# The router product of a two-layer encoder: router as stationary operand, plain fp32 in place of three split products

## The reference, cut to what matters

```python
y = h * rsqrt(mean(h * h) + 1e-6) * g2        # RMSNorm, 1024 frames
logits = y @ w_router                          # (1024, 1024) @ (1024, 8)
top_val, top_idx = top_k(logits, 2)
gates = softmax(top_val)
# each frame goes through the SwiGLU of its two experts (inner width 3584),
# y_e = (silu(y @ Wg[e]) * (y @ Wu[e])) @ Wd[e], weighted by its gates
```

## Time and profile before

| what | value |
|---|---|
| median of 3 runs | 4281.76 us (4280.26 to 4285.87) |
| span of the profiled execution | 4292.7 us |
| own time of the profiled execution | the page gives its span alone |
| busy: TensorE | 3891.8 us (91%) |
| busy: VectorE, ScalarE | 1811.8 us (42%), 1699.0 us (40%) |
| mean granted TensorE clock | 0.936 |

### The profile page before, as it was taken

How to read it: one execution, slowest core, us unless ns; L and a number is a source line. 1 busy time by engine, 2 the same in 40 slices (tenths; PEclk the granted TensorE clock), 3 DMA queues, 4 the chain that set the end, 5 groups by cost and what they waited for, 6 DMA issues and landing times.

```text
span 4292.7 us, 69381 instructions
## 1 busy us (share of the span) xinstructions
PE 3891.8 (91%) x25092; PEld 3517.8 (82%) x25093; DVE 1811.8 (42%) x2616; ACT 1699.0 (40%) x2513; POOL 91.9 (2%) x118
## 2 busy tenths in 40 slices
PE   7888888999999998996599898998999999998994
PEld 5777776688778866875599898997999999998994
DVE  4443434333243233323244453553444545454444
ACT  3333333333233232213354453543545555464543
POOL 1000000000000000001000000000000000000001
PEclk8889878999999999996799999999999999999997
DMA  4000001133323331112545455554555656565556
GB/s 147 26 26 28 23 20 64 61 96 93 93 73 93 93 108 50 34 64 45 143 156 170 151 182 166 185 195 137 164 175 172 197 192 196 193 196 180 167 166 227
DMA packets 149206, 530.78 MB, mean 124 GB/s; under 512 B 17816, under 2 KB 17856, under 8 KB 148752
## 3 DMA queue, kind: packets, MB, share of 16 engines
q1 hardware_dynamic: 126864, 461.95, 33.8%
q0 software_dynamic: 12864, 49.22, 3.3%
q10 hardware_dynamic: 9280, 17.24, 1.3%
HBM read 501.88 MB, written 30.14 MB: 124 GB/s over the span
## 4 chain that ended last, share of the span: by engine, by line
PE 86%; DVE 5%; issue 4%; ACT 2%; DMA 1%; ACTq 0%; POOL 0%; DVEq 0%; POOLq 0%
PE ps L255 28%; PE ps L257 27%; PE ps L256 27%; PE ps L304 1%; PE ps L395 1%; DMA hrow_d<-rows 1%; DVE rstd L286 1%; DVE tb L295 1%; DVE ptl L452 0%; PE ps L961 0%; DMA y<-yrow_d,slot 0%; DVE xl L503 0%; DVE xl L291 0%; ACT prob L472 0%; DVE prob L424 0%
## 5 line engine op out<-in xcount | busy, mean ns | idle before, releaser
L250 DVE TENSOR_TENSOR wl<-wraw,wh 128x1024 fp32r<-128x1024 f32 x864 | 1057.2, 1224 | 1644.8 <-ACT wh L246 1644.5
L246 ACT ACTIVATE wh<-wraw 128x1024 fp32r<-128x1024 f32 x864 | 909.2, 1057 | 1227.4 <-PE ps L257 1219.2
L255 PE MATMUL ps<-exh,wh 128*128 128x240 f32 (+3 forms) x3584 | 1031.3, 288 | 103.9 <-issue 94.2
L256 PE MATMUL ps<-exl,wh 128*128 128x240 f32 (+3 forms) x3584 | 1029.4, 287 | 0.6 <-issue 0.6
L257 PE MATMUL ps<-exh,wl 128*128 128x240 f32 (+3 forms) x3584 | 1029.3, 287 | 0.0
L255 PEld LDWEIGHTS ps<-exh,wh 128*128 128x128 f32 x3584 | 685.0, 191 | 106.1 <-issue 106.1
L257 PEld LDWEIGHTS ps<-exh,wl 128*128 128x128 f32 x3584 | 684.4, 191 | 0.8 <-issue 0.8
L256 PEld LDWEIGHTS ps<-exl,wh 128*128 128x128 f32 x3584 | 684.9, 191 | 0.0
L255 PE MATMUL ps<-mah,wh 128*128 (+4 forms) x1792 | 511.6, 285 | 0.6
L257 PE MATMUL ps<-mah,wl 128*128 (+4 forms) x1792 | 510.8, 285 | 0.0
L256 PE MATMUL ps<-mal,wh 128*128 (+4 forms) x1792 | 510.8, 285 | 0.0
(11 more groups left out here) (234 smaller groups left out, 4837.7 us busy)
## 6 DMA issues: line engine op xcount, KB each, us to landing
wraw<-in_w_expert SPq DMA_DIRECT2D x676, 512.0 KB, 3.4
wraw<-in_w_main SPq DMA_DIRECT2D x188, 512.0 KB, 3.6
yrow_d<-yst ACTq DMA_DIRECT2D x16, 512.0 KB
yT<-in_xT POOLq DMA_DIRECT2D x4, 1024.0 KB, 10.6
hT<-in_xT POOLq DMA_DIRECT2D x1, 4096.0 KB, 13.8
h_d<-hT POOLq DMA_DIRECT2D x1, 4096.0 KB, 13.2
hT<-h_d POOLq DMA_DIRECT2D x1, 4096.0 KB, 12.5
xrow_d<-rows ACTq DMA_DIRECT2D x16, 256.0 KB
```

The costliest lines, as they stand in the source:

```text
L246: act.activation(wh[:, j], wraw[:, j], ACT.Copy).then_inc(hi_done, 1)
L250: dve.tensor_tensor(wl[:, j], wraw[:, j], wh[:, j].bitcast(F32), ALU.subtract).then_inc(lo_done, 1)
L255: pe.matmul(out, a_hi, b_hi, start=first, stop=False)
L256: pe.matmul(out, a_hi, b_lo, start=False, stop=False)
```

## The change

The router block (128 channels x 8 experts) becomes the stationary operand and 512 normed frames move, in plain fp32, straight from `yT`: 16 instructions, 8 for each half, with the logits as 8 partitions x 512 frames in bank 6 (half 0) and bank 4 (half 1). VectorE copies both to the new tile `lgT`; after batch 1 of the row transposes TensorE turns `lgT` back with 8 transposes into bank 6, where the logits stand as before. The high and low parts of the normed frames and of the router are not made any more; the tiles `rwh`, `rwl` and the semaphores `r_hi`, `r_lo` go. ScalarE takes the root of half 0 before the squares of half 1, and TensorE waits block by block (`n_t`) rather than for the last low part.

```diff
--- before.py
+++ after.py
@@ -149,7 +149,7 @@
         s4 = ExitStack()
         sb("under_norm", [P, 3 * KD * T + 6 * HALF], F32, s4)
         rw = sb("rw", [P, KD * NE], F32, s4)
-        rwh, rwl = (sb(n, [P, KD * NE], F32R, s4) for n in ("rwh", "rwl"))
+        lgT = sb("lgT", [NE, T], F32, s4)
         below = sb("below", [P, P], F32, s4)
         tokid = sb("tokid", [P, NT], U32, s4)
         iota8 = sb("iota8", [P, NT, NE], F32, s4)
@@ -217,7 +217,7 @@
         sc, ttr, ex, es, st2, pn = (sem(n) for n in ("sc", "ttr", "ex", "es", "st2", "pn"))
         tr, pt_hi, pt_lo, pv, y_a, y_d = (sem(n) for n in ("tr", "pt_hi", "pt_lo", "pv", "y_a", "y_d"))
         sp_hi, sp_lo, h_in, op_mm, op_add = (sem(n) for n in ("sp_hi", "sp_lo", "h_in", "op_mm", "op_add"))
-        r_in, r_hi, r_lo, lg_mm, lg_cp, r_own, rk_mm = (sem(n) for n in ("r_in", "r_hi", "r_lo", "lg_mm", "lg_cp", "r_own", "rk_mm"))
+        r_in, lg_mm, lg_cp, r_own, rk_mm = (sem(n) for n in ("r_in", "lg_mm", "lg_cp", "r_own", "rk_mm"))
         g_exp, r_cst, slots_ok, items_ok, tok_z, tok_st = (sem(n) for n in ("g_exp", "r_cst", "slots_ok", "items_ok", "tok_z", "tok_st"))
         tr_mm, row_cp, row_st = sem("tr_mm"), sem("row_cp"), [sem(f"row_st{b}") for b in range(ROWS)]
         list_in, x_got, xt_mm, x_hi, x_lo = (sem(n) for n in ("list_in", "x_got", "xt_mm", "x_hi", "x_lo"))
@@ -799,14 +799,14 @@
         def route_pe(pe):
             norm_pe(pe, 6)
             norm_pe(pe, 7)
-            pe.wait_ge(r_lo, 1)
-            for t in range(NT):
-                pe.wait_ge(n_lo, 56 if t < NT // 2 else 64)
-                c = slice(t * P, t * P + P)
+            pe.wait_ge(r_in, 16)
+            for half in range(2):
+                c = slice(half * HALF, half * HALF + HALF)
                 for k in range(KD):
-                    e = slice(k * NE, k * NE + NE)
-                    mm = product(pe, bank(6, NE, t * NE), xh[:, k, c], xl[:, k, c], rwh[:, e], rwl[:, e], k == 0, k == KD - 1)
-            mm.then_inc(lg_mm, 1)
+                    pe.wait_ge(n_t, 8 * (6 + half) + k + 1)
+                    mm = pe.matmul(bank((6, 4)[half])[0:NE], rw[:, k * NE:k * NE + NE], yT[:, k, c],
+                                   start=k == 0, stop=k == KD - 1)
+                mm.then_inc(lg_mm, 1)
             for b in range(32):
                 if b >= 4:
                     pe.wait_ge(row_cp, b - 3)
@@ -814,6 +814,11 @@
                 for i in range(4):
                     mm = pe.transpose(bank(b % 4, P, P * i), src[:, 4 * (b % 2) + i, b % 16 // 2 * P:b % 16 // 2 * P + P], ident[:])
                 mm.then_inc(tr_mm, 1)
+                if b == 1:
+                    pe.wait_ge(lg_cp, 2)
+                    for t in range(NT):
+                        mm = pe.transpose(bank(6, NE, t * NE), lgT[:, t * P:t * P + P], ident[0:NE, 0:NE])
+                    mm.then_inc(lg_mm, 1)
                 if b == 5:
                     pe.wait_ge(r_own, R_SENT)
                     pe.matmul(bank(5, NT * NE), below[:], sent[:].rearrange("p t e -> p (t e)"), start=True, stop=False)
@@ -822,12 +827,12 @@
 
         def route_act(act):
             act.wait_ge(op_add, 32)
-            squares_act(act, 6, hT, 0)
-            squares_act(act, 7, hT, 1)
-            norm_act(act, 6, 0, xdst(0), yT)
-            norm_act(act, 7, 1, xdst(1), yT)
-            act.wait_ge(r_in, 16)
-            act.activation(rwh[:], rw[:], ACT.Copy).then_inc(r_hi, 1)
+            for half in range(2):
+                n = 6 + half
+                squares_act(act, n, hT, half)
+                act.wait_ge(n_squ, 8 * n + 8)
+                act.wait_ge(n_rstd, n)
+                act.activation(rs[:], sums(n), ACT.Sqrt, bias=epsc[:, 0:1], scale=1.0 / D).then_inc(n_rs, 1)
             for b in range(32):
                 t = b % 16 // 2
                 act.wait_ge(tr_mm, b + 1)
@@ -842,10 +847,19 @@
                               rows[:, b % ROWS]).then_inc(row_st[b % ROWS], 16)
 
         def route_dve(dve):
-            norm_dve(dve, 6, hT, 0, 3, xdst(0), yT)
-            norm_dve(dve, 7, hT, 1, 3, xdst(1), yT)
-            dve.wait_ge(r_hi, 1)
-            dve.tensor_tensor(rwl[:], rw[:], rwh[:].bitcast(F32), ALU.subtract).then_inc(r_lo, 1)
+            for half in range(2):
+                n = 6 + half
+                cols = slice(half * HALF, half * HALF + HALF)
+                dve.wait_ge(n_rs, n + 1)
+                dve.wait_ge(n_t, 8 * n)
+                dve.reciprocal(rstd[:], rs[:]).then_inc(n_rstd, 1)
+                dve.wait_ge(n_rstd, n + 1)
+                for k in range(KD):
+                    dve.scalar_tensor_tensor(yT[:, k, cols], hT[:, k, cols], gains[:, 3, k:k + 1], rstd[:],
+                                             ALU.mult, ALU.mult).then_inc(n_t, 1)
+            for half in range(2):
+                dve.wait_ge(lg_mm, half + 1)
+                dve.tensor_copy(lgT[:, half * HALF:half * HALF + HALF], bank((6, 4)[half])[0:NE]).then_inc(lg_cp, 1)
             n = [0]
 
             def own(ins):
@@ -853,7 +867,7 @@
                 n[0] += 1
                 ins.then_inc(r_own, 1)
                 dve.wait_ge(r_own, n[0])
-            dve.wait_ge(lg_mm, 1)
+            dve.wait_ge(lg_mm, 3)
             dve.wait_ge(r_cst, 5)
             own(dve.tensor_copy(lg[:].rearrange("p t e -> p (t e)"), bank(6, NT * NE)))
             for t in range(NT):
```

## The result

The changed kernel takes 4216.49 us in the median (4213.56 to 4222.31, 4 runs) against 4283.18 for the kernel before, measured again beside it in 4 runs; the ratio is 0.9838, 95% interval 0.9825 to 0.9851: 66.7 us less, where 52.2 were predicted.

The account below looks back on a forecast made before the run. Bound: router stage, 30.1 us of TensorE idle while VectorE makes blocks, then a 41.2 us product at clock 0.50. Norm, product and turning back bring the logits 52.2 us earlier: 4281.8 - 52.2 = 4229.6 us, range 4216 to 4248.

Parts of the forecast that it names:

- The stage: Router stage from the norm's squares to the logits' copy: logits can be copied 52.2 us earlier, at 1959.7 instead of 2011.90.
- Turning back: After the router product: eight transposes of `lgT` on TensorE, bounded by 0.7 and 2.6 us, taken as 1.3.
- faster than summed: Rival, router product: 8-column weight loads and ready blocks remove its gap, ending up to 4.4 us sooner; 4225, 8%.
- The bound for the low clock: Router product at low clock throughout, 30.2 us, ending 1972.3; as a rival 34.3 us saved, 4247.5, 12%.
- The clock: Router product: TensorE comes from the sums without a break and stays at 1.00, 0.93 us an instruction.
- an 8-column side loses the clock: Rival, router product: 8-column stationary side leaves the clock low from about its start; 34.3 us saved, 4247.5, 12%.
- The join: List load, where row stream (about 54 us earlier) meets the tokens' path (52.2): the later one's shift, 52.2, counts.
- The experts: Experts' stretch after the router: expected to stay as long as the 2195.8 us of before.
- a smaller drift of the same kind: Experts' items: pauses at their starts may shift by 10 us in all either way, kept in the range.
- slower than before: Rival, experts' item starts: shorter code moves what follows; all eight pauses at 21.6 cost 78.4 us more, 4308.0; 3%.
- the floor case: Router product ends at VectorE's floor, up to 4.4 us sooner; 4225, 8%; with a drift of 9 the range's bottom.

Follow-up runs that it names:

- product_only: Changed kernel with the norm of before: both roots after both halves' squares, high and low parts still made; 4250.1 us, ratio 0.9916.
- frames_stationary: Changed kernel with the product's sides swapped back, 128 frames stationary and 8 router columns moving, plain fp32, no lgT; 4224.6 us, ratio 0.9860.
- pad_act: Changed kernel with 15 more semaphore increments on ScalarE before its row copies, nobody waiting for them; 4232.1 us, ratio 0.9877.
- before_act113: Kernel before the change with 113 semaphore increments added on ScalarE, while it idles during the router product; 4268.7 us, ratio 0.9963.

## Why the prediction was wrong

**The stage, right.** 52.2 us were summed, 54.4 measured. By steps, from the first square: root of half 0, 8.3 us predicted, 8.3 measured; first blocks at 12.4 and 12.4; last block of half 1 at 26.8 and 26.7; product's end 32.1 and 30.9; logits' copy 34.8 and 32.6. The product was sized at the 0.466 us a record of the norm's sums, and it runs at 0.434:

```profile
L807 PEld LDWEIGHTS ps<-yT,rw x32: 85/90/90, 1933.9 to 1946.8; 128*8 128x8 f32 x32
L807 PE MATMUL ps<-yT,rw x32: 592/592/596, 1934.0 to 1947.3; 128*8 128x512 f32 x32
```

The weight loads of 8 columns take 0.09 us instead of the sums' 0.19, and the blocks are all there when their turn comes; which of the two closes the gap no run separates. Turning back took 0.65 us instead of 1.3. Both errors lie between the bounds given, towards the rival that was called "faster than summed". There was one table load, no drain and no second load, as forecast (1923.95, 1.28 us, root at 1925.24). The bound for the low clock was read from a weak row: 1.89 us an instruction, in a stretch for which the profile shows no low clock; product_only gives 1.70 at 0.50. The sum did not use it.

**The clock, right, though the reason given was thin.** The rival (an 8-column side loses the clock) did not come true, 1.00 throughout. frames_stationary shows that it does come true for 8 moving columns: 22.30 us of a busy TensorE, and the clock fell. The Trainium skill, page "TensorE: Matmul & The Clock Gate", Part 1, ties the full clock to sustained busyness; in frames_stationary busyness alone did not hold it, so the measurement decides.

**The join, right.** The list load waited 12.91 us for the scatter before and 12.47 after; from the logits to the first turned row it is 56.8 us instead of 57.0. What the stage gains arrives at the experts whole, within the 82.5 to 85.3 us that the way there takes in any of the traces.

```profile
1991.79 0.81 POOL L960 DMA_DIRECT2D tokl<-tok_d  x1 [12.47 <-DMA tok_d<-tokid,slot]
```

**The experts, wrong: this is the step that failed.** The prediction took the pauses at the items' starts as they were, with "a smaller drift of the same kind, 10 us in all either way". It looked at TensorE's own pauses "for nothing shown", and those hardly moved; the changed kernel's line is

```profile
L255 PE MATMUL ps<-exh,wh 128*128 128x240 f32 (+3 forms) x3584 | 1028.6, 287 | 97.1 <-issue 95.6
```

94.2 us became 95.6. What moved was ScalarE's start, and it shows in the rest of that line, TensorE's waits for weights: 103.9 less 94.2 is 9.7 us before, 97.1 less 95.6 is 1.5 after. With the products slowed by the clock behind these waits it is about 13 us in items 6 and 7, shown by pad_act and before_act113 to hang on where ScalarE's code lies. The rival "slower than before" had the mechanism (the code behind the edit lies elsewhere) with the opposite sign and on another engine. 54.4 + 13 = 67 accounts for the 66.7 of the medians. The remaining 9.7 us between the two traces are the 8.0 ahead of the router and the 1.6 between logits and experts, by which executions of one program differ as well. That the median of 4216.49 us itself lies inside 4216 to 4248 is no merit: the range ended where a drift of 9 us on top of the floor case would have put it, and the drift was 13 with nearly the forecast stage.

What stays open: why the first square comes anywhere between 1916 and 1931 in executions of kernels that are the same up to there, and which of ScalarE's branches crosses which boundary.

## What to carry to other kernels

When an operand of a product is narrow, try it as the stationary one: here the wide one then streamed, the loads were half as long, and the clock stayed at 1.00. That was the smaller part, 6.7 of 54.4 us; dropping the three split products and the work that split their operands gave the rest. Ahead of a loop with large branches, count each engine's instructions before and after an edit: this kernel of straight-line stages and branched code won or lost some 0.3% by where the code behind the edit lay, and that is easily taken for the edit's merit; padding one engine at a time in its idle time tells the two apart. Look for a code pause on every engine that feeds the loop, not on the busiest alone.

## What the runs showed of the hardware that was not expected

- 113 instructions that do nothing made a kernel faster by 15.2 us (0.9963, 0.9950 to 0.9975); 15 such instructions cost another 10 to 16 us, by which kernel it is compared with.
- The step of ScalarE from one item to the same code of the next took 4.24 or 11.05 us, with 4 or 10 packets of 8 KB on queue q14 around it.
- The pause of 4.3 us that this gave TensorE was followed by 6.8 us at a granted clock of 0.50, so that it cost 7.4 us in all.
- TensorE fell from a granted clock of 1.00 to 0.50 while busy for all of 22.30 us, with 8 moving columns.
- A plain fp32 stream of 512 columns ran at 0.434 us a record with 8 stationary columns and at 0.466 with 128 in the norm's sums, where weight loads are 0.19 us and squares arrive one by one.
